# A two-layer hybrid trunk: norms and the embedding gate merged into the stages around them, and the first mixer started tile by tile

## The reference

```python
for i in range(DEPTH):                      # DEPTH = 2
    h = rmsnorm(x, norm_mix[i])
    x = x + (even_mixer(h, ...) if i % 2 == 0 else mlstm_mixer(h, ...))
    x = x + peer(rmsnorm(x, norm_ffn[i]), pk_w_q[i], pk_sub_k1[i], pk_sub_k2[i], pk_u[i], pk_v[i])
    gate = jax.nn.sigmoid(rmsnorm(x, norm_ple[i]) @ ple_gate[i])
    x = x + gate * (p[i] @ ple_w[i])
return rmsnorm(x, norm_final)
```

## Time and profile before

| | us |
|---|---|
| median of 3 runs | 4397.84 (4397.66 to 4400.72) |
| profiled execution | 4396.69 |
| its span, first to last instruction | 4395.2 |
| TensorE busy | 4265.2 (97%) |
| VectorE busy | 2725.5 (62%) |
| ScalarE busy | 2082.4 (47%) |
| GpSimd busy | 1234.4 (28%) |
| mean granted clock of TensorE | 0.987 of 2.4 GHz |

### The profile page before, as it was taken

The page is one execution under the profiler, slowest core; times in us unless marked ns, Lnnn a source line. Parts: engine busy times, 40 slices in busy tenths (PEclk is TensorE's granted clock), DMA queues, the critical chain, the costliest instruction groups (busy, mean ns, idle before and its releaser), DMA issues. The chain is left out here.

```text
span 4395.2 us, 61439 instructions
## 1 busy us (share of the span) xinstructions
PE 4265.2 (97%) x19295; PEld 3449.9 (78%) x19295; DVE 2725.5 (62%) x5660; ACT 2082.4 (47%) x4061; POOL 1234.4 (28%) x1571
## 2 busy tenths in 40 slices
PE   7999999999999999999899999999999999999997
PEld 5665787888888888887688887888888888888884
DVE  3546699777774444444577764997778744444444
ACT  2655333677773333333455553335777833333324
POOL 0210245777760000000100001447788700000000
PEclk9999999999999999999899999999999999999998
DMA  2111233555557565642222222335555575555531
GB/s 102 58 48 34 95 111 134 197 192 183 202 214 254 180 211 176 210 172 86 67 85 86 86 85 87 114 127 183 191 195 185 205 263 190 192 197 189 200 106 58
DMA packets 178197, 653.99 MB, mean 149 GB/s; under 512 B 17200, under 2 KB 17328, under 8 KB 172928
## 3 DMA queue, kind: packets, MB, share of 16 engines
q1 hardware_dynamic: 100944, 371.41, 24.9%
q0 software_dynamic: 40240, 213.69, 13.7%
q10 hardware_dynamic: 36864, 67.13, 4.1%
HBM read 507.42 MB, written 144.74 MB: 148 GB/s over the span
## 5 line engine op out<-in xcount | busy, mean ns | idle before, releaser
L184 PE MATMUL ps<-h_hi,w_hi 128*128 128x512 f32 x4232 | 1669.3, 394 | 58.2 <-PEq L280 34.0
L184 PE MATMUL ps<-h_hi,w_lo 128*128 128x512 f32 x4232 | 1653.4, 391 | 0.0
L184 PE MATMUL ps<-h_lo,w_hi 128*128 128x512 f32 x4232 | 1653.2, 391 | 0.0
L163 DVE TENSOR_TENSOR w_lo<-w_raw,w_hi 128x1024 fp32r<-128x1024 f32 x585 | 718.9, 1229 | 1057.7 <-ACT w_hi L157 1053.7
L157 ACT ACTIVATE w_hi<-w_raw 128x1024 fp32r<-128x1024 f32 x694 | 734.7, 1059 | 1023.7 <-PE ps L184 859.9
L184 PEld LDWEIGHTS ps<-h_hi,w_hi 128*128 128x128 f32 x4232 | 797.3, 188 | 237.4 <-issue 45.3
L184 PEld LDWEIGHTS ps<-h_hi,w_lo 128*128 128x128 f32 x4232 | 797.1, 188 | 169.4
L184 PEld LDWEIGHTS ps<-h_lo,w_hi 128*128 128x128 f32 x4232 | 797.7, 188 | 158.3 <-issue 2.1
L1623 POOL TENSOR_SCALAR second_hot<-iota,token_keys 128x128 fp32r<-128x128 f32 x1024 | 723.3, 720 | 0.0
L1661 ACT ACTIVATE first_scaled<-first_hot,token_keys 128x128 fp32r<-128x128 f32 x1792 | 539.2, 388 | 0.4 <-DVE first_scaled L1593 0.4
L184 PE MATMUL ps<-y_hi,w_hi 128*128 128x512 f32 x1216 | 483.7, 398 | 11.8 <-DVE y_lo L384 9.9
(11 more groups left out here) (331 smaller groups left out, 3552.9 us busy)
## 6 DMA issues: line engine op xcount, KB each, us to landing
w_raw<-in_u SPq DMA_DIRECT2D x256, 512.0 KB, 3.3
w_raw<-in_v SPq DMA_DIRECT2D x256, 512.0 KB, 3.3
gates<-gate_group POOLq DMA_DIRECT2D x36, 2048.0 KB, 7.9
acts<-gelu ACTq DMA_DIRECT2D x256, 256.0 KB, 2.1
gate_block<-gates POOLq DMA_DIRECT2D x32, 2048.0 KB, 17.9
gelu_block<-acts POOLq DMA_DIRECT2D x30, 2048.0 KB, 11.6
w_raw<-in_od_in SPq DMA_DIRECT2D x65, 512.0 KB, 3.3
w_raw<-in_ev_in SPq DMA_DIRECT2D x33, 512.0 KB, 3.3
```

What stands on the lines that cost most here:

```text
L163: self.nc.vector.tensor_tensor(self.wl[:, slot % SPL, :], self.raw[:, slot, :], self.wh[:, slot % SPL, :].bitcast(F32), ALU.subtract).then ...
L184: ins = self.nc.tensor.matmul(out, a[:, s, w], b[:, k, :], start=first and j == 0 and m == 0, stop=last and j == n - 1 and m == 2)
```

## The change

1. **Start.** The residual is loaded in 8 transfers, one per tile, between the first weight units; the parameters and the first unit are issued ahead of them. The separate `norm` is gone: EvenFront holds a `Norm` and multiplies its first unit tile by tile as OddMixer does. All 34 products of EvenFront are multiplied with `rstd` as they leave PSUM, all by VectorE (early ones instead of copying, late ones in `evict`, which moves from ScalarE to VectorE). The early units use four banks instead of two.
2. **Embedding and gate.** Class `Ple` replaces `Embedding`, `ple_gate` and their blocks, and runs in the block of the feed-forward part. During the last 8 units of Values, ScalarE and VectorE split the finished tiles of the residual and square them. GpSimd sums the squares (`pool_sums`), and TensorE does a single matmul with ones (`pe_total`) after the first embedding unit. The gate's products are scaled by VectorE, and ScalarE's sigmoid follows in SBUF.
3. **Last norm.** The squares for it are taken and summed as the gate's tiles are added; then come one matmul, root, reciprocal and 8 scalings, and each tile is stored by its own transfer as soon as it is scaled.

The core of the diff:

```diff
@@ start
-            sp.dma_start(p.x[:, :, :], p.dram["x"]).then_inc(ld.sem, 16)
             sp.dma_start(p.par[:, :], p.dram["par"]).then_inc(ld.sem, 16)
-            prefetch(p, sp, nxt)
-            sp.wait_ge(ld.sem, 32)
+            prefetch(p, sp, nxt[:1])
+            for k in range(DK):
+                sp.dma_start(p.x[:, k, :], p.dram["x"][:, k, :]).then_inc(p.sig(f"x_loaded{k}").sem, 16)
+                if k in (3, 5, 7):
+                    prefetch(p, sp, nxt[k // 2:k // 2 + 1], p.unit + k // 2)
+            sp.wait_ge(ld.sem, 16)
@@ class Norm
+    def pool_sums(self, pool):
+        for k in range(1, DK):
+            pool.wait_ge(self.sq.sem, self.sq.at(k + 1))
+            if k > 1:
+                pool.wait_ge(self.sa.sem, self.sa.at(k - 1))
+            self.p.nc.gpsimd.tensor_tensor(self.total, self.s2[:, 0, :] if k == 1 else self.total,
+                                           self.s2[:, k % 2, :], ALU.add).then_inc(self.sa.sem, 1)
+    def pe_total(self, pe):
+        p = self.p
+        pe.wait_ge(self.sa.sem, self.sa.at(DK - 1))
+        p.nc.tensor.matmul(p.ps[:, self.bank, :], p.ones[:, :], self.total, start=True, stop=True
+                           ).then_inc(self.ss.sem, DK)
@@ class EvenFront
+            if n == 0:
+                self.norm.pe_unit(pe, u0, p.ps[:, self.EARLY_BANK[0], :])
+                continue
@@ EvenFront.scalar
-        for n in range(len(EARLY)):
+        for k in range(DK):
+            act.wait_ge(p.sig(f"x_loaded{k}").sem, 16)
+            self.norm.act_tile(act, k)
+            if k == 3:
+                ahead(0)
+        self.norm.act_root(act)
+        for n in range(1, len(EARLY)):
             ahead(n)
@@ EvenFront.evict
-        p.nc.scalar.activation(dst, p.ps[:, 7, :], ACT.Copy).then_inc(self.late_out.sem, 1)
+        p.nc.vector.tensor_tensor(dst, p.ps[:, 7, :], self.norm.rstd, ALU.mult).then_inc(self.late_out.sem, 1)
@@ EvenFront.vector
+        for k in range(DK):
+            self.norm.dve_tile(dve, k)
+            if k == 3:
+                ahead(0)
+        self.norm.dve_root(dve)
+        rstd = self.norm.rstd
         for n, i in enumerate(EARLY):
-            ahead(n)
+            if n:
+                ahead(n)
             dve.wait_ge(used.sem, u0 + n + 1)
...
             for n in self.units(e):
                 ahead(n)
+                if e == -2:
+                    self.evict(dve, n)
...
+            if e > -2:
+                self.evict(dve, self.units(e)[0])
@@ Values, last block
+                else:
+                    self.after.act_early(act, j)
...
+                    self.after.dve_early(dve, j)
                     dve.wait_ge(used.sem, u0 + i * B + j + 1)
-                    p.nc.vector.tensor_tensor(p.x[:, j, :], p.ps[:, j, :], p.x[:, j, :], ALU.add)
+                    p.nc.vector.tensor_tensor(p.x[:, j, :], p.ps[:, j, :], p.x[:, j, :], ALU.add
+                                              ).then_inc(self.added.sem, 1)
@@ class Ple
+    def act_early(self, act, j):
+        if j:
+            act.wait_ge(self.values.added.sem, self.values.added.at(j))
+            self.norm.act_tile(act, j - 1)
...
+    def sync(self, sp):
...
+        if self.final:
+            for k in range(DK):
+                sp.wait_ge(self.fin.sem, self.fin.at(k + 1))
+                sp.dma_start(p.dram["out"][:, k, :], p.x[:, k, :]).then_inc(self.stored.sem, 16)
+    def scalar(self, act):
...
+        split(1)
+        act.wait_ge(self.values.added.sem, self.values.added.at(DK))
+        self.norm.act_tile(act, DK - 1)
+        take(0)
+        self.norm.act_root(act)
+        split(2)
+        for n in range(1, 4):
+            take(n)
+        for n in range(4, DK):
+            take(n)
+            if n == 4:
+                split(3)
+        for i in range(DK):
+            split(4 + i) if 4 + i <= 2 + DK else None
+            act.wait_ge(self.sc.sem, self.sc.at(i + 1))
+            a.activation(self.sg[:, i, :], self.sg[:, i, :], ACT.Sigmoid).then_inc(self.si.sem, 1)
+            if self.final and i:
+                act.wait_ge(self.ad.sem, self.ad.at(i))
+                self.last.act_tile(act, i - 1)
+    def vector(self, dve):
...
+        split(1)
+        self.norm.dve_tile(dve, DK - 1)
+        split(2)
+        self.norm.dve_root(dve)
+        split(3)
+        for i in range(DK):
+            if 4 + i <= 2 + DK:
+                split(4 + i)
+            dve.wait_ge(used.sem, u0 + 3 + i)
+            v.tensor_tensor(self.sg[:, i, :], p.ps[:, 2 + i % 2, :], self.norm.rstd, ALU.mult).then_inc(self.sc.sem, 1)
+            if i:
+                add(i - 1)
+        add(DK - 1)
```

More of the change, by code:

```diff
@@ new lines, in tensor @@
+            ins.then_inc(used.sem, 1)
+            if j == 0:
+                self.norm.pe_total(pe)
+        pe.wait_ge(self.norm.nl.sem, self.norm.nl.at(DK))
+        for i in range(DK):
+            if i < 2:
+                pe.wait_ge(self.et.sem, self.et.at(2 + i))
+            else:
+                pe.wait_ge(self.sc.sem, self.sc.at(i - 1))
+            p.product(pe, u0 + 2 + i, (u0 + 2 + i) % RAW, p.ps[:, 2 + i % 2, :], p.yh, p.yl).then_inc(used.sem, 1)
+        if self.final:
+            self.last.pe_total(pe)
@@ L2369, in ffn_firsts, with ffn @@
     return firsts(d[f"wq{layer}"])
-def ffn(p, layer, nxt):
+def ffn(p, layer, nxt, final=None):
     d = p.dram
@@ L2399, in ffn @@
                             [pw_[0, :, :], pw_[1, :, :], gate[0, :, :], gate[1, :, :]], c)
-        together(p, topk, decode, gates, values)
-    with ExitStack() as ctx:
-        pw = p.sb("embedded", [P, DK, T], ctx=ctx)
-        sg = p.sb("ple_gate", [P, DK, T], ctx=ctx)
-        embedding = Embedding(p, pw, p.sb("embedding", [P, 2, T], ctx=ctx), d["emb"][layer])
-        p.unit += RAW
-        norm(p, p.x, f"norm_ple{layer}", out=(p.hh, p.hl), nxt=[gate[2, :, :], gate[3, :, :]], beside=embedding)
-        p.unit -= RAW
-        embedding.done()
-        ple_gate(p, gate, pw, sg, nxt)
+            ple = Ple(p, values, d["emb"][layer], gate, f"norm_ple{layer}", nxt, c, final)
+        together(p, topk, decode, gates, values, ple)
 def trunk(nc, dram):
```

345 lines of the change are left out of this document (113 added, 232 removed).

## The result

| | before | after |
|---|---|---|
| median, us | 4398.07 (4397.66 to 4400.72, 4 executions) | 4335.07 (4331.72 to 4336.64, 4 executions) |
| ratio of the mean times, 95% interval | | 0.9854 (0.9837 to 0.9872) |
| profiled execution: time, span | 4396.69, 4395.2 | 4336.64, 4335.1 |

What follows compares the result with a forecast made beforehand. TensorE, busy in 97% of 4395.2 us, was taken as the bound, so only its idle time could be won. Terms 21.8 - 1.8 - 0.1 + 20.8 - 1.3 - 0.5 + 20.7 + 8.9 = 68.5 led to 4329, range 4321 to 4341.

Steps and rivals of the forecast that it cites:

- rival (1): Seams: splits pushed back by 3 us in both layers, TensorE then returning at half rate, 4340; 14%.
- (2): Start bound by its transfers: first weight unit or first tiles land late, 3.5 us lost, 4333; 10%.
- Start: Program start: third unit begins at 33.7 instead of 55.5, 21.8 us won, less 1.8 for the clock.
- the term of 1.8 for the clock in TensorE's pause: Ahead of the third unit: 2.6 us of idling lowers TensorE's clock; 1.8 taken between 0 and 2.4.
- rival (3): TensorE stays at full rate in the 2.6 us start pause and the end is not held, 4326; 20%.
- Evictions: Even mixer: TensorE's restart after the first late unit loses 0.1 us; in later steps other matmuls hide it.
- Seams: Values to gate in each layer: 55.35 us instead of 76.2 and 76.05, winning 20.8 and 20.7.
- The narrow room of 0.6 us: First gate unit: its split ends at 11.2 us after Values, 0.6 us before TensorE needs it.
- Odd start: Layer 0, into the odd mixer: 1.3 us lost behind the last gate unit, 0.5 for longer half rate.
- End: Last gate matmul to the end of the span: 22.0 us instead of 30.9, so 8.9 won.
- The hold: End: GpSimd's sum of tile 6 may hold VectorE's last addition, ending it at 4.8 instead of 3.6 us.
- Everything else is untouched: Experts and the mixers' middle: no change expected, apart from the late evictions of the first mixer.

Runs made afterwards that it cites:

- third_early: Changed kernel with both halves of the third unit's split ahead of the root on ScalarE and the reciprocal on VectorE; 4330.51 us, ratio 0.9846.
- evict_twice: Changed kernel with every late eviction done twice by VectorE, one behind the other; 4339.54 us for one execution.
- start_only: Kernel before with only the changed start, first norm and even mixer front; embedding, gate and end as before; 4380.59 us, ratio 0.9962.
- adds_early: Changed kernel with VectorE adding the previous tile ahead of its wait for the current gate unit; 4336.28 us, ratio 0.9860.
- the two pad kernels: Changed kernel with 24 or 12 tiny extra ScalarE copies in the even front; 4330.72 and 4330.66 us, ratio 0.9846 each.
- seams_only: Changed kernel with the start, first norm and even mixer front of the kernel before; 4348.28 us, ratio 0.9886.

## Why the prediction was right, and what it missed

The time lay in the range and the forecast's mechanism was the one that happened; its sum was 8.4 us too high, nearly all of it (7.3) from stages that it had left out. That the time still lies in the range is owed to the range's upper end, which had been set for rivals (1) and (2), and neither of them happened: no seam stalled, and the block opened near its forecast. The terms below are measured on TensorE's rows of the two profiled executions.

**Start: 20.0 net forecast, 20.8 measured** (the split at 61.00 came at 40.18). Block at 8.3 (8.74), second unit at 25.7 (25.90), third at 33.7 (34.35). Each was 0.2 to 0.7 us late, and the term of 1.8 for the clock in TensorE's pause was nothing here: 2.38 us left the clock at 1.00, the part of rival (3) that came true. That was luck. The same pause cost 1.6 us of clock in four of the nine profiles that have it, near the 1.8, and nothing in five. I had taken one price from the length of the pause ("nearer to 3.39"); the length alone doesn't set it. third_early shows that the pause itself was avoidable.

**Evictions: -0.1 forecast, -0.1 measured** (0.78 us against 0.69). evict_twice shows the cover: complete in the later steps even for a longer one, almost none beyond the single eviction in the first three.

**Seams: 20.8 and 20.7 forecast, 20.6 and 20.45 measured,** and in the table the first one is the same within 0.05 us in ten kernels. The narrow room of 0.6 us was 0.64 by the trace and 0.5 by experiment; rival (1) had the place right and the price wrong. Contention between the two engines was there (GpSimd's sums took 1.85 us, the subtraction for the embedding's low part 2.31 where a split of the same shape takes 1.23), and had cover.

**Odd start: -1.3 and -0.5 forecast, -3.0 measured.** This is the term inside the sum that was mis-sized most. The idle time grew by 1.0 (5.34 against 4.34), near the 1.3; the clock took 2.0 and not 0.5: 1.5 in the first unit (16.7 us to the second unit's first matmul at 2125.99, against 15.3), since half rate lasted about twice as long, and 0.5 further on. start_only, with 4.35 us of idling, lost 1.4 there too, and kernels with 5.70 lost 2.8 to 3.5 in the table's column, no more than the 3.5 of the changed kernel, so the length isn't a clean function of the idle time; what sets it stays open. start_only's 1.41 won at the first seam, where its program is the kernel before's, is the same thing the other way: behind the same pause of 8.1 us ahead of the gate, half rate ended 3 us sooner.

**End: 8.9 forecast, 8.6 measured.** The hold was foreseen, but with the victim exchanged: I let GpSimd hold VectorE's addition, and here VectorE slowed GpSimd's sum. adds_early then showed the case that I had described. The eight stores took 2.2 us from issue to landing (median), near the 2.1 of the row that the sum went by and not the 2.6 of the estimate beside it. The Trainium skill, "GPSIMD Engine Reference", section Specifications, says that GpSimd contends with VectorE instructions that have two SBUF inputs. The rows agree, and they show it in two directions: 0.69 to 1.65 on VectorE, 1.27 to 1.71 on GpSimd here and to 1.85 at the seam.

**Outside the sum: -3.7 in EvenSSD, -2.9 in Gates, -0.7 from the odd mixer on.** "Everything else is untouched" was the step that failed. The work was untouched; the position of ScalarE's code was not, and gate 0 paid 2.9 us for it (the two pad kernels). EvenSSD's loss comes without the new start too (seams_only), at different sizes in every kernel (0.5 to 4.6); that it is the execution's and not the change's is likely, but no profile of the kernel before has shown it. The last 0.7 is a sum. TensorE's pause of 3.26 us at 2673.31 left the clock at 1.00, where the kernel before fell to 0.50 behind its 2.96 (1.3 won); the one of 2.11 us at 2902.17 was followed by 0.50, where the kernel before kept 1.00 (0.8 lost); and the Gates loop of layer 1 lost 1.3 by its position. Why the clock has several courses is open. The medians differ by 63.0 and the profiles by 60.1 because the profiled execution of the changed kernel was 1.6 above its median and that of the kernel before 1.4 below.

## What to carry to other kernels

When one engine is full, price a change in its idle times only, and read the room of the narrowest wait from the trace; such a sum came out within 0.3 us per seam. Don't take one price for a pause's clock from one row: the same pause had two. Then look at the loops behind: taking instructions from an engine's queue moves the code of every later loop, and the idle row marked "issue" one instruction behind a loop's head shows it; here 12 or 24 tiny instructions in an idle place cured it. Where GpSimd and VectorE both read SBUF, the one that comes second pays, so keep GpSimd out of the last microseconds ahead of a result.

## What the runs showed of the hardware that was not expected

- The same pause of TensorE, 2.4 us ahead of the third unit, was followed by a granted clock of 1.00 in five kernels and of 0.50 in four (35 to 37 us). One of 3.26 us was followed by 1.00 in the changed kernel (2675 to 2677 us) and by 0.50 in adds_early (2673.5 to 2675.5). The pauses of 0.56 to 1.51 us above cost at most 0.2 us beyond themselves.
- The same start pattern of the odd mixer ran at half rate for about 3 us in the kernel before and 6 in the changed one (windows of 1.00 and 0.61 above).
- At the head of each pass of the Gates loop ScalarE stands for 3.5 to 3.7 us in which it waits for nothing that the profile shows, and in the kernels with 915 of its instructions ahead for 0.82 to 1.11 more one instruction later; TensorE, one unit ahead, loses about 0.95 for that each time.
- A 128x512 addition on VectorE with both inputs in SBUF took 0.69 us alone and 1.65 beside a GpSimd sum that began 0.16 us before it.
- The matmul of 128x512 with ones took 1.02 us at full rate and 2.05 at half rate.
